# A decoder layer in split fp32 on one core: the FFN's up projection by Strassen's seven block products, its activations kept in DRAM, and the down projection as a phase of its own

## The reference, cut to what matters

```python
x = x + merged @ w_out[layer]
h = rms_norm(x, ffn_norm_g[layer])
u, v = jnp.split(h @ w_up[layer], 2, axis=-1)      # w_up (2048, 11264)
u = causal_dwconv(u, conv_w[layer], conv_b[layer])  # 3 taps along the tokens
x = x + (jax.nn.gelu(u) * v) @ w_down[layer]        # w_down (5632, 2048)
...
return rms_norm(x, final_norm_g)
```

## Time and profile before

| | |
|---|---|
| timed executions | 2839.16, 2839.32, 2840.89 us; median 2839.32 |
| span of the profiled execution | 2837.4 us |
| PE busy | 2813.3 us, 12777 matmuls |
| PEld busy | 2321.8 us |
| DVE busy | 1104.6 us |
| ACT busy | 801.0 us |
| POOL busy | 178.7 us |
| moved by DMA | 277.29 MB, 98 GB/s |

### The profile page before, as it was taken

The page is one execution under the profiler, slowest core; times in us unless marked ns, Lnnn a source line. Parts: engine busy times, 40 slices in busy tenths (PEclk is TensorE's granted clock), DMA queues, the critical chain, the costliest instruction groups (busy, mean ns, idle before and its releaser), DMA issues.

```text
span 2837.4 us, 32306 instructions
## 1 busy us (share of the span) xinstructions
PE 2813.3 (99%) x12777; PEld 2321.8 (82%) x12777; DVE 1104.6 (39%) x1332; ACT 801.0 (28%) x910; POOL 178.7 (6%) x156
## 2 busy tenths in 40 slices
PE   8999999999999999999999999999999999999998
PEld 6888888888888888888888888888888888888886
DVE  4345542233333333332434343434434343434344
ACT  4334432222232322233422222222212122222223
POOL 0013310000111000000000000000000000000002
PEclk9999999999999999999999999999999999999999
DMA  6432223333323233342333333333232323333332
GB/s 174 133 102 56 66 69 96 99 97 97 96 78 90 81 104 89 104 148 89 113 95 101 92 102 90 98 94 100 92 102 90 103 89 92 100 95 97 96 96 104
DMA packets 404586, 277.29 MB, mean 98 GB/s; under 512 B 4757, under 2 KB 365862, under 8 KB 403897
## 3 DMA queue, kind: packets, MB, share of 16 engines
q1 hardware_dynamic: 400391, 268.56, 32.8%
q10 hardware_dynamic: 3714, 6.56, 0.7%
q0 software_dynamic: 432, 1.50, 0.2%
HBM read 272.36 MB, written 6.33 MB: 98 GB/s over the span
## 4 chain that ended last, share of the span: by engine, by line
PE 95%; issue 1%; ACT 1%; DMA 1%; DVE 1%; SPq 0%; POOL 0%; ACTq 0%; DVEq 0%; POOLq 0%
PE bank L411 30%; PE bank L413 30%; PE bank L412 30%; PE bank L602 2%; PE bank L596 1%; DMA x<-in_x_dram 1%; DMA x_in<-in_x_dram 0%; ACT l_win L936 0%; ACT l_slc L936 0%; PE bank L652 0%; PE bank L751 0%; POOL l_slc L1574 0%; SPq L313 0%; DVE h_lo L1390 0%; DVE w_lo L1154 0%
## 5 line engine op out<-in xcount | busy, mean ns | idle before, releaser
L411 PE MATMUL bank<-h_hi,w_hi 128*128 128x512 f32 x2624 | 1030.1, 393 | 3.0 <-DVE w_lo L1164 3.0
L413 PE MATMUL bank<-h_hi,w_lo 128*128 128x512 f32 x2624 | 1022.9, 390 | 0.0
L412 PE MATMUL bank<-h_lo,w_hi 128*128 128x512 f32 x2624 | 1022.5, 390 | 0.0
L1154 DVE TENSOR_TENSOR w_lo<-w_raw,w_hi 128x2048 fp32r<-128x2048 f32 x237 | 543.8, 2294 | 485.4 <-ACT w_hi L838 472.9
L838 ACT ACTIVATE w_hi<-w_raw 128x2048 fp32r<-128x2048 f32 x237 | 452.4, 1909 | 749.0 <-PE bank L413 748.6
L411 PEld LDWEIGHTS bank<-h_hi,w_hi 128*128 128x128 f32 x2624 | 493.3, 188 | 103.0 <-issue 3.6
L413 PEld LDWEIGHTS bank<-h_hi,w_lo 128*128 128x128 f32 x2624 | 492.8, 188 | 103.1
L412 PEld LDWEIGHTS bank<-h_lo,w_hi 128*128 128x128 f32 x2624 | 493.2, 188 | 99.1
L411 PE MATMUL bank<-w_hi,a_hi 128*128 128x512 f32 x704 | 274.1, 389 | 0.0
L412 PE MATMUL bank<-w_lo,a_hi 128*128 128x512 f32 x704 | 274.1, 389 | 0.0
L413 PE MATMUL bank<-w_hi,a_lo 128*128 128x512 f32 x704 | 274.1, 389 | 0.0
(11 more groups left out here) (242 smaller groups left out, 1932.5 us busy)
## 6 DMA issues: line engine op xcount, KB each, us to landing
w_raw<-in_w_up_dram SPq DMA_DIRECT2D x88, 1024.0 KB, 5.7
w_raw<-in_w_in_dram SPq DMA_DIRECT2D x76, 1024.0 KB, 5.6
w_raw<-in_w_down_dram SPq DMA_DIRECT2D x44, 1024.0 KB, 5.1
w_raw<-in_w_out_dram SPq DMA_DIRECT2D x16, 1024.0 KB, 5.1
w_raw<-in_w_branch_nsa_dram SPq DMA_DIRECT2D x8, 1024.0 KB, 5.3
w_raw<-in_w_branch_fox_dram SPq DMA_DIRECT2D x8, 1024.0 KB, 5.3
x_in<-in_x_dram SPq DMA_DIRECT2D x4, 1024.0 KB, 11.1
x<-in_x_dram ACTq DMA_DIRECT2D x4, 1024.0 KB, 10.8
```

The source lines that it names most:

```text
L411: mm(dst, l_hi, r_hi, start=first, stop=False)
L412: mm(dst, l_hi, r_lo, start=False, stop=False)
L413: return mm(dst, l_lo, r_hi, start=False, stop=final)
L1154: V.tensor_tensor(w_lo[:, s.par, :], w_raw[:, s.par, :], w_hi[:, s.par, :].bitcast(F32), ALU.subtract).then_inc(w_ready, 1)
```

## The change

**Up projection.** Unit n (44 of them) is u's 128 columns n and v's 128 columns n together: a matrix of 256 columns, which meets y (2048 x 512 tokens, the normed activations without the per-token factor). Both are cut in two along the contraction, y also along the tokens, and W into v and u. That is one level of the 2x2 scheme in its form with seven products (Strassen's, with shared sums). Each product is a `product` of 8 blocks times 3 matmuls, 256 tokens wide. The seven left factors of a unit ("pieces") are v's two halves, u's second half and four sums and differences (`s_a` as s1, s2, s4 in turn, and `s_3`), which DVE computes per unit. Then ACT and DVE split each piece into `ring_hi` and `ring_lo`, a ring of 4. The right factors y11, y21, y22 and four differences t1 to t4 are computed and split once, ahead of and during the first ten products. `piece_ok` counts finished pieces and `prod_done` finished products. A piece may be split once the product four before is done. Unit r's last two products (u's second half and s4) stand in the period of unit r+1. Five reads of PSUM per unit (`out_c11`, `out_c12`, `out_c22`, `out_c21`, ACT's `p1`, `p5`, `u2`) put the blocks of u and v together in SBUF.

**Hidden activations.** Convolution and gelu run one or two periods later over one `conv_t`. POOL multiplies by v, and SP stores the 128x512 result to `a_dram`.

**Down projection.** It has 11 chunks of 4 slots, all after the up projection. A chunk's activations are loaded back (1 MB), split by ACT and DVE (128x2048 each), and the 128x512 matmuls are as before, with the same count. The per-token factor is applied where DVE adds a bank to `x1` (a scalar_tensor_tensor in place of a tensor_tensor). `x1` itself is stored to `x1_dram` group by group, and loaded again after the last product.

**Out projection.** ACT loads x by groups (`load_xr`), and the wait for it stands inside `wo_add`.

```diff
+        def product(q, b, y_hi, y_lo, bank, first):
+            pe.wait_ge(piece_ok, q + 1)
+            for k in range(KH):
+                w = slice(k * P, k * P + P)
+                for left, right in ((ring_hi[b], y_hi), (ring_hi[b], y_lo), (ring_lo[b], y_hi)):
+                    last = mm(pb[bank][:, 0:TH], left[:, w], right[:, k, :], ...)
+            last.then_inc(prod_done, 1)
...
+            product(now.q, b, y11_hi, y11_lo, bank_a[par], True)
+            pe.wait_ge(c11_out, now.n)
+            product(now.q + 1, (b + 1) % RING, y21_hi, y21_lo, bank_b, True)
...
+            product(now.q + 2, (b + 2) % RING, t1_hi, t1_lo, bank_c[par], True)
+            pe.wait_ge(p1_out, now.n + 1)
+            product(now.q + 3, (b + 3) % RING, t2_hi, t2_lo, bank_a[par], False)
+            pe.wait_ge(c22_out, now.n)
...
+            product(now.q + 4, b, t4_hi, t4_lo, bank_a[1 - par], False)
...
+            pe.wait_ge(p5_out, now.n)
+            product(now.q + 5, (b + 1) % RING, y22_hi, y22_lo, bank_c[1 - par], False)
+            pe.wait_ge(u2_out, now.n + 1)
+            product(now.q + 6, (b + 2) % RING, t3_hi, t3_lo, bank_a[par], False)
```

ACT's part of a piece, and SP's order around the end of the up projection:

```diff
+        def piece(q, b, src):
+            if not isinstance(q, int) or q >= RING:
+                act.wait_ge(prod_done, q - (RING - 1))
+            A(ring_hi[b][:], src, ACT.Copy).then_inc(piece_hi, 1)
...
+        load_a(0, 0)
+        load_a(1, 1)
+        store_a(unit(41))
+        sp.wait_ge(prod_done, PRODUCTS)
+        sp.wait_ge(x1_put, 80)
         for j in range(4):
+            sp.dma_start(x1[:, :, 512 * j:512 * j + 512], x1_d[:, :, 512 * j:512 * j + 512]).then_inc(x_loaded[j], 16)
+        store_a(unit(42))
+        store_a(unit(43))
+        sp.wait_ge(a_out, 16 * UNITS + 64)
...
+                    hold(sp, w_ready, s.n + 1)
+                    load_down(s, c, j)
```

More of the change, by code:

```diff
@@ new lines, in _, with chunk_loads @@
+        sp.wait_ge(a_out, 16 * UNITS + 64)
+        def chunk_loads(c, par, per, i, first, last):
+            for j in range(4):
+                s = slot(S_DN + 4 * par + j, per, i)
+                if not (first and j < 2):
+                    hold(sp, w_ready, s.n + 1)
+                    load_down(s, c, j)
+                if j == 3 and not last:
+                    hold(sp, a_ok, c + 1)
+                    load_a(c + 2, par % 2)
+        for par in range(2):
+            chunk_loads(par, par, 0, None, par == 0, False)
@@ L795, in down_slots @@
[L795 to L812, removed]
@@ L1080, in _, with y_hi_part, piece_x @@
-        hi(slot(S_U0 + 1))
+        def y_hi_part(dst, src, adds=None):
+            if adds is not None:
+                act.wait_ge(t_add, adds)
+            A(dst, src, ACT.Copy).then_inc(yh_part, 1)
+        def piece(q, b, src):
+            if not isinstance(q, int) or q >= RING:
+                act.wait_ge(prod_done, q - (RING - 1))
+            A(ring_hi[b][:], src, ACT.Copy).then_inc(piece_hi, 1)
+        def piece_x(q, b, m, row, half):
+            if row == 0:
+                act.wait_ge(n0_in[m.r % 2], m.half * 16 + 16)
+            else:
+                act.wait_ge(n1_in[m.r % 2], m.half * 32 + 32)
+            piece(q, b, raw[m.r % 2][row][:, half, :])
@@ new lines, in _, with down_hi, a_high @@
+        period(1)
+        with act.Fori(0, 10) as i:
+            for r in range(2, 6):
+                period(r, i)
+        period(42)
+        period(43)
+        def down_hi(s):
+            act.wait_ge(w_loaded[s.par], s.half * 16 + 16)
+            act.wait_ge(w_used, s.n + 1)
+            A(d_hi[:, s.par, :], d_raw[:, s.par, :], ACT.Copy).then_inc(w_hi_done, 1)
+        def a_high(c, ap, loads):
+            act.wait_ge(a_loaded[ap], loads)
+            A(a_hi[ap][:], a_in[ap][:], ACT.Copy).then_inc(ah_ok, 1)
@@ L1468, in _, with y_lo_part, piece, x_of @@
-        lo(slot(S_U0 + 1))
-        dve.wait_ge(x1_put, 4 * TOK + 1)
+        def y_lo_part(nth, dst, src, high):
+            dve.wait_ge(yh_part, nth)
+            V.tensor_tensor(dst, src, high.bitcast(F32), ALU.subtract).then_inc(y_part, 1)
+        def piece(q, b, src):
+            dve.wait_ge(piece_hi, q + 1)
+            V.tensor_tensor(ring_lo[b][:], src, ring_hi[b][:].bitcast(F32), ALU.subtract).then_inc(piece_ok, 1)
+        def x_of(m, row, half):
+            return raw[m.r % 2][row][:, half, :]
```

635 lines of the change are left out of this document (456 added, 179 removed).

## The result

The changed kernel takes 2806.97 us (median of 4, 2806.79 to 2808.48) against 2839.24 for the kernel before: a ratio of 0.9884, with a 95% interval of 0.9872 to 0.9896. That is 32.3 us less, where 54.8 less were forecast. The forecast was 2785, and 2806.97 lies in its range of 2760 to 2820.

What follows compares the result with a forecast made beforehand. PE, busy 99% of the span, was taken to bound the kernel. Matmuls -91.6, out projection -1.2, start +24 and end +14 make -54.8 us, from the median of 2839.3 to 2785, range 2760 to 2820.

Steps and rivals of the forecast that it cites:

- Matmul pace: Up projection: 7392 matmuls of 256 columns at 117.1 ns (bounds 113.3 and 120) replace 4224 at 226.6, saving 91.6 us.
- Weight loads: Up projection: PE can take a full load every 110 ns, so loads stay hidden at 117.1, a margin of 7 ns.
- the rule cited there: Skill page: loads overlap matmuls only when row groups differ; each new load would be bare, 107 ns more per matmul.
- Rival (e): Up projection: the load under 256 columns doesn't hide in a long run; gain gone from 124.5 ns a matmul; chance 0.03.
- DVE: Steady up projection: DVE's 17.1 us a unit hide behind PE's 19.7, so steady periods are charged nothing.
- rival (d): Up projection: DVE becomes the bound, gain gone at 20.9 us a unit; 2840 to 3000 us; chance 0.08.
- Out projection: DVE's wait for the loads of x moves behind the low parts: -1.2 us.
- Start: Start of the up projection: PE waits for factors and pieces made on DVE and ACT, +24 us (bounds 18 and 34).
- the 2.4 us that were added for half clock: Start of the up projection: one product at half clock where DVE waits for it, part of the +24.
- End: End of the up projection: waits for piece 306 and the third down slot, +14 us (bounds 6 and 20).
- Rival (c): FFN loop: its code no longer stays on PE and is fetched at each return, 2805 to 2835 us; chance 0.08.
- Rival (b): Up projection: both ends cost half, or the pace is half a 512 matmul's, 2745 to 2765 us; chance 0.13.

Runs made afterwards that it cites:

- b256: Kernel before, with 84 of its 88 up slots cut into two passes of 256 columns, same sums: 2906.6 us, ratio 1.0235.
- n64: Changed kernel, each product loading only 64 of each block's 128 weight columns, with 256 moving columns: 2759.73 us (one run).
- dve2: Changed kernel with two more sums of 128x1024 on DVE in each unit: 2832.52 us, ratio 0.9974 to the kernel before.
- dve4: Changed kernel with four more sums of 128x1024 on DVE in each unit: 2943.59 us, ratio 1.0366 to the kernel before.
- entry_pool: Changed kernel with two of the right factors' sums at the start on POOL instead of DVE: 2811.15 us, ratio 0.9899 to the kernel before.
- exit_pieces: Changed kernel with the first down slot's and first chunk's halves on DVE and ACT moved behind pieces 306 and 307: 2802.53 us.
- exit_load: Changed kernel with the third down slot's load issued ahead of the loads of x1: 2797.61 us, ratio 0.985 to the kernel before.
- exit_both: Changed kernel with the edits of exit_pieces and exit_load together: 2791.57 us, ratio 0.9829 to the kernel before.
- w128: Changed kernel, each product streaming 128 instead of 256 token columns, half the tokens left out: 3485.81 us (one run).
- all: Changed kernel with the edits of exit_both and entry_pool together: 2795.6 us, ratio 0.984 to the kernel before.

## Why the prediction was right, and where it was off

**Matmul pace: right mechanism, one term mis-sized.** The step is "I take 117.1, from the longer run". The changed kernel runs at 120.0, the upper bound that was given: 7392 x 2.9 ns = 21.4 us less saved, -70.2 instead of -91.6. That is nearly the whole distance from 54.8 to 32.3. The earlier trace rows has 66 weight columns, half the shape that was asked for. The earlier trace rows has the right shape and was read as 120 ns, but its times are rounded to 0.01 us: in the trace's own nanoseconds its two matmuls stand 118 and 117 apart, and all sixteen such pairs in the kernel before give 116 to 118. So no row of 256 columns in the kernel before shows 120.0; only the long runs of the changed kernel and of b256 do. But the prediction's own first figures held the answer: 226.6 is 213.3 for the columns and 13.3 beside them, and with 13.3 kept whole, 256 columns give 106.7 + 13.3 = 120.0. Half of 226.6, the lower bound, would need the 13.3 to halve as well. b256 shows that neither the shorter products nor DVE's new work makes the pace: the kernel before gives it too, when cut. That a change of the weights' shape moves the pace is shown by n64; why 32 and 66 columns are slower than 64, why a pair of full ones is faster than a long run, and why 224 moving columns have more than 13.3 beside them, is open. No experiment here tells what the chip does in that time.

**Weight loads** hide, as forecast against the rule cited there: no matmul of the steady part stands more than 121 ns from the next, with a load each. Rival (e) is out.

**DVE.** 17.1 us a unit were forecast, 16.2 measured (668.74 us in 830, units of 20.16), and no wait of PE in the steady periods, as forecast; dve2 and dve4 put the room at about 2 us where the prediction had 2.6 (19.7 less 17.1). That the two are close is partly luck: the busy time was overrated, and it was not seen that DVE waits for ACT's high parts in every unit (164 times, 125.2 us), which was the mechanism of rival (d). These waits fitted into PE's time. Rival (d)'s break-even of 20.9 us held in dve2. The transfers for u came late once, by 0.4 us.

**Out projection.** -1.2 forecast, -1.4 found.

**Start.** +24 forecast, 20.7 found. The chain of steps held closely: products 1, 2, 3, 4 and 9 start 8.0, 13.7, 18.6, 32.0 and 49.0 us after the first, where 8.0, 14.0, 18.6, 32.1 and 49.5 were worked out. entry_pool shows from the other side that DVE sets these times: a slower DVE moved products 2 and 3 by 4.3 and 7.5 us. The step that was off is the 2.4 us that were added for half clock. Products 1 and 4 did run in part at half clock (24 matmuls about 213 ns apart, 2.2 us more), but product 9 still waited 1.1 us for its piece: the slow matmuls fell into time that PE would have spent waiting.

**End.** +14 forecast, 18.4 found. The wait of piece 306 is 6.6 for 6.5, and exit_pieces took it down to 2.2 by the order alone. The third down slot waits 7.9 us, not 5.2, and then runs at half clock, 2.1 more, which the prediction did not charge here. Its load is issued 17.6 us after the last product (forecast 14.5). The timeline of SP in the changed kernel, and the time to landing of the last two stores (14.1 and 12.9) and of one later load (9.5):

```profile
2303.66 2.21 SPq L490 DMA_DIRECT2D x<-x_dram  x4
2305.99 3.56 SPq L441 DMA_DIRECT2D a_dram<-v_sb  x2
2321.07 0.94 SPq L472 DMA_DIRECT2D d_raw<-in_w_down_dram  x2
```

```profile
DMA to landing us min/median/max: 9.5/12.9/14.1
```

A store of 0.25 MB lands in 2.0 us elsewhere (page, the median of 44); the last ones, issued behind 4 MB of x1, take 14.1 and 12.9, and SP waits for them before it issues the down slot's load. The prediction had 13.0 us for x1 and 1.5 for what follows. It left out a load of another engine that runs in the same time, 1 MB for the final norm's gain:

```profile
2307.72 0.61 POOL L1976 DMA_DIRECT2D gfin<-in_final_norm_g_dram  x1
```

From 2304 to 2322 us the DMA engines move 5.8 MB, of which x1 and the two stores are 4.7. At the 400 GB/s of the earlier trace rows the other 1.05 MB take 2.6 us, most of the 3.1 us by which the load is issued late. That is an estimate; no run moved this load. That SP's order makes the stall is shown by exit_load: with the down slot's load ahead of x1 the time is 9.4 us less, against 7.9 + 2.1 = 10.0 at this place.

**Rival (c)**, the loop's code, did not happen, and b256 shows that it was a real one, at 1.5 us a return instead of 2 to 5. **Rival (b)** asked for both ends at half their price or the pace at 113.3, and got neither. That the errors of the two ends (-3.3 and +4.4) cancel is luck; the forecast missed by the pace.

Of the two kernels and the variants that compute the whole result exit_both is the fastest: 2791.57 us, 1.7% under before.

## What to carry to other kernels

Split a matmul's measured pace into its columns at the granted clock and a rest before you scale it. Here the scheme halved the columns, kept a load per matmul and kept the rest, 13.3 ns. The rest is no constant, though (6.6 to 18.3 in the table above), and a pair of matmuls does not show what a long run takes: time the very shape in a run of some hundreds before you trust a margin of 3 ns. An eighth fewer column-passes became 7.3% less time in these matmuls (887.0 of 957.2 us). And where two phases meet, go through each engine's order by hand: two moved pieces of code there gave back 15 of the 39 us that the new scheme cost at its ends. A busy share overrates the room on an engine that waits for another in every round: 3.9 us of idle on DVE held 2 us of work.

## What the hardware showed that was not expected

- At half clock a 256-column matmul takes 213.3 ns, its columns at 1.2 GHz and nothing beside them. With 128 moving and 128 weight columns it takes 213.3 as well (w128), and the clock stayed at 0.50 over the 1590 us of the projection, nearly all of it without a pause, while 224 and 256 columns (1.00) rose from the same gaps.
- The pace at 256 moving columns is lowest at 64 weight columns (113.3 ns), with 117.7 at 32 and 120.0 at 128. Pairs with 128 weight columns take 117, long runs 120.0.
- A loop body of 960 matmuls stalls PE 1.4 to 1.7 us at each return, one of 672 doesn't.
- POOL's sum over 128x2048 stretched the DVE subtraction beside it by 4.3 us; in dve2 its product over 128x512 stretched one subtraction of each unit by 1.1.
- Behind the same pause of 2.2 us the clock fell in exit_pieces and all (0.94 from 2270 to 2300 us) and stayed at 1.00 in exit_both.
